# A mixer layer's TensorE stream rewritten: transposed projections, one attention slot per pair, and the softmax division on VectorE

## What is computed

```
(qa, ka, va, za, qb, ckv, iq, ik, iw, zb, qc, kc, vc, zc, ga, gb, gc) = _split_cols(h @ w_in[l])
ckv = _rmsnorm(ckv, ckv_g[l])
ya = _mixer_a(qa, ka, va, sink[l], t5_bias) * jax.nn.silu(za)
yb = _mixer_b(qb, ckv, iq, ik, iw, w_uk[l], w_uv[l], t5_bias) * jax.nn.silu(zb)
yc = _mixer_c(qc, kc, vc, c_rel_bias[l]) * jax.nn.silu(zc)
merged = (jax.nn.sigmoid(ga) * (ya @ w_pa[l]) + jax.nn.sigmoid(gb) * (yb @ w_pb[l])
          + jax.nn.sigmoid(gc) * (yc @ w_pc[l]))
x = x + merged @ w_o[l]
return _rmsnorm(x, final_g)
```

## Time and profile before

| what | value |
|---|---|
| median of 3 runs | 1018.62 us |
| lowest, highest | 1018.24, 1019.21 us |
| the profiled execution's own time | 1018.98 us |
| its span | 1017.2 us |
| mean granted TensorE clock | 0.996 of full |
| busy: TensorE, VectorE, ScalarE, GpSimd | 98%, 56%, 46%, 10% |
| moved by DMA | 187.01 MB, mean 184 GB/s |

### The profile page before, as it was taken

The page is one execution under the profiler, slowest core; times in us unless marked ns, Lnnn a source line. Parts: engine busy times, 40 slices in busy tenths (PEclk is TensorE's granted clock), DMA queues, the critical chain, the costliest instruction groups (busy, mean ns, idle before and its releaser), DMA issues.

```text
span 1017.2 us, 14153 instructions
## 1 busy us (share of the span) xinstructions
PE 1001.8 (98%) x4835; PEld 827.3 (81%) x4835; DVE 573.2 (56%) x954; ACT 469.8 (46%) x757; POOL 101.3 (10%) x125
## 2 busy tenths in 40 slices
PE   8999999999999999999999999999999999999995
PEld 6887888888888888888888888888888888888884
DVE  6656555555655555655645557566456545545652
ACT  6554444444444445543544455445434434444441
POOL 1000211111110300221211002211000000000000
PEclk9999999999999999999999999999999999999998
DMA  9765555555555555555556555555455865555452
GB/s 307 243 207 172 172 180 187 169 173 160 164 175 175 176 166 176 188 174 175 161 184 182 166 176 187 169 174 164 156 195 166 316 220 188 189 181 186 166 197 92
DMA packets 106218, 187.01 MB, mean 184 GB/s; under 512 B 12752, under 2 KB 24096, under 8 KB 105536
## 3 DMA queue, kind: packets, MB, share of 16 engines
q1 hardware_dynamic: 105792, 186.21, 57.0%
q0 software_dynamic: 240, 0.24, 0.1%
q10 hardware_dynamic: 144, 0.01, 0.0%
HBM read 184.26 MB, written 2.17 MB: 183 GB/s over the span
## 4 chain that ended last, share of the span: by engine, by line
PE 97%; DMA 1%; DVE 0%; SPq 0%; issue 0%; ACT 0%; POOLq 0%; DVEq 0%; POOL 0%
PE bank L1010 29%; PE bank L1012 29%; PE bank L1011 28%; PE bank L984 4%; PE bank L1033 2%; PE bank L1147 1%; PE bank L1049 1%; PE bank L1050 1%; PE bank L1048 1%; DMA raw<-in_w_in_dram 1%; PE bank L1122 0%; SPq L329 0%; PE bank L1086 0%; PE bank L1085 0%; PE bank L1084 0%; DVE act L975 0%
## 5 line engine op out<-in xcount | busy, mean ns | idle before, releaser
L703 DVE TENSOR_TENSOR w_lo<-raw,w_hi 128x1024 fp32r<-128x1024 f32 (+1 forms) x324 | 400.8, 1252 | 279.9 <-ACT w_hi L502 278.5
L1010 PE MATMUL bank<-w_hi,h_hi 128*128 128x512 f32 x1088 | 436.0, 401 | 2.5 <-DVE w_lo L703 2.5
L502 ACT ACTIVATE w_hi<-raw 128x1024 fp32r<-128x1024 f32 (+1 forms) x324 | 336.0, 1050 | 209.2 <-PE bank L1012 190.6
L1012 PE MATMUL bank<-w_hi,h_lo 128*128 128x512 f32 x1088 | 425.0, 391 | 0.0
L1011 PE MATMUL bank<-w_lo,h_hi 128*128 128x512 f32 x1088 | 423.7, 389 | 0.0
L1010 PEld LDWEIGHTS bank<-w_hi,h_hi 128*128 128x128 f32 x1088 | 204.4, 188 | 44.6 <-issue 3.1
L1012 PEld LDWEIGHTS bank<-w_hi,h_lo 128*128 128x128 f32 x1088 | 204.2, 188 | 44.1
L1011 PEld LDWEIGHTS bank<-w_lo,h_hi 128*128 128x128 f32 x1088 | 204.7, 188 | 39.6
L438 POOL TENSOR_TENSOR biasmask<-bias,masks 128x512 f32<-128x512 f32 (+1 forms) x48 | 65.2, 1378 | 245.3 <-DMA bias<-bias_table 241.0
L1010 PE MATMUL bank<-w_hi,y_hi 128*128 128x512 f32 x192 | 76.4, 398 | 0.0
L1012 PE MATMUL bank<-w_hi,y_lo 128*128 128x512 f32 x192 | 75.0, 390 | 0.0
(11 more groups left out here) (152 smaller groups left out, 578.8 us busy)
## 6 DMA issues: line engine op xcount, KB each, us to landing
raw<-in_w_in_dram SPq DMA_DIRECT2D x232, 512.0 KB, 4.3
raw<-in_w_o_dram SPq DMA_DIRECT2D x32, 512.0 KB, 4.2
raw<-in_w_pa_dram SPq DMA_DIRECT2D x16, 512.0 KB, 3.6
raw<-in_w_pb_dram SPq DMA_DIRECT2D x16, 512.0 KB, 3.6
raw<-in_w_pc_dram SPq DMA_DIRECT2D x16, 512.0 KB, 4.5
bias<-bias_table SPq DMA_DIRECT2D x24, 256.0 KB, 4.9
raw<-in_w_in_dram SPq DMA_DIRECT2D x16, 256.0 KB, 5.9
act<-in_x_t_dram SPq DMA_DIRECT2D x8, 256.0 KB, 6.4
```

The source lines that it names most:

```text
L502: nc.scalar.activation(w_hi[:, s, 0:n], raw[:, s, 0:n], ACT.Copy).then_inc(hi_ready, 1)
L703: nc.vector.tensor_tensor(w_lo[:, s, 0:n], raw[:, s, 0:n], w_hi[:, s, 0:n].bitcast(F32), ALU.subtract).then_inc(lo_ready, 1)
L1010: mm(acc, xh, wh[:, e, :], start=first, stop=False)
L1012: ins = mm(acc, xl, wh[:, e, :], start=False, stop=last)
```

## The change

All loops are unrolled, and pieces come in a new order, packed on the host into one array `w_s` (4 KB contiguous per partition and piece); biases with branch A's and C's masks are laid out on the host too, one load of 393 KB per pair.

- `CHUNKS`: q, z, k of branch C and the indexer's q are computed transposed (`cols_step`): weights stationary, 128 columns, and 256 columns of h moving; a piece is 4 k-tiles by 256 output columns (2 by 512 for iq), 24 products. The expansion of the latent (uk, uv) becomes streamed pieces. There are 330 pieces: g 96, q 48, z 48, P 48, o 32, k 16, v 16, kvc 8, iq 8, ik 4, uk 4, uv 2; those of uk have 12 products of 256.
- `slots`: TensorE attends once per pair, in slot i after a given piece: P times V of pair i-1, scores of pair i+1, transposes of pair i. P times V has v (64 columns) stationary and 128 columns of P's transpose moving, so y comes out transposed, one head on each half of the partitions. Slots stand 6 to 16 pieces apart.
- VectorE divides the probabilities by their sum before they are transposed (4 `tensor_scalar` per pair), and multiplies P times V by the SiLU path when it leaves PSUM.
- The first two chunks use x scaled by the gain alone; for the rest x is multiplied by the norm's factor on GpSimd (`x_scaled`), where also the sums of squares are added and the power of a 128 by 256 row tile is taken, and split again on ScalarE and VectorE.
- The first piece is loaded and split in halves; x's first part comes by ScalarE's queue; the warm-up is 13 products of 512.

The diff, cut to its core:

```diff
-BR = 10
-KINDS = ["q", "q", "i"] + ["q"] * 10 + ["z", "z", "g", "P", "g", "P", "g", "P", "g", "P"] * 3 + ["o"] * 4
-PIECES = [8, 8, 4] + [8] * 10 + [8, 8, 8, 4, 8, 4, 8, 4, 8, 4] * 3 + [8] * 4
+CHUNKS = ([("kvc", 0, 0), ("iq", 0, 0), ("ik", 0, 0)] + quarters("q", 0) + quarters("z", 0)
+          + [k for u in range(4) for k in (("q", 1, u), ("uk", 0, u))]
+          + [("q", 2, 0), ("uv", 0, 0), ("q", 2, 1), ("uv", 0, 1), ("q", 2, 2), ("q", 2, 3)]
+          + quarters("k", 0) + [("v", 0, 0), ("v", 0, 1)] + quarters("z", 1)
+          + branch(0) + quarters("z", 2) + branch(1) + branch(2) + quarters("o", 0))
+KINDS = [k for k, _, _ in CHUNKS]
+PIECES = [{"uk": 1, "uv": 1, "kvc": 8, "iq": 8, "v": 8, "g": 8, "o": 8}.get(k, 4) for k in KINDS]
...
+def slots():
+    yield -1, FIRST[AT["z", 0, 3]]
+    for i, key in enumerate((("q", 1, 0), ("q", 1, 2), ("q", 2, 0), ("q", 2, 2), ("k", 0, 0), ("k", 0, 2),
+                             ("v", 0, 0), ("v", 0, 1))):
+        yield i, FIRST[AT[key]] + 2
+    for b in range(2):
+        yield 8 * b + 8, FIRST[AT["z", b + 1, 0]] + 2
+        for k in range(7):
+            yield 8 * b + 9 + k, FIRST[AT["g", b, 0]] + 2 + 6 * k
+    yield 24, FIRST[AT["g", 2, 0]] + 1
...
+            def parts(g, n):
+                return [w[:, g % RING, 0:width(g)].rearrange("p (k n) -> p k n", n=n) for w in (w_hi, w_lo)]
+            def cols_step(g, c, e, kt, n_kt, hi_t, lo_t):
+                n_blk = 4 if KINDS[c] == "iq" else 2
+                wh, wl = parts(g, n_blk * P)
+                for n in range(n_blk):
+                    cols = slice(n * P, (n + 1) * P)
+                    acc = bank[2 * (c % 2) + n][:, 0:SEQ]
+                    mm(acc, wh[:, e, cols], hi_t[:, kt, :], start=kt == 0, stop=False)
+                    mm(acc, wh[:, e, cols], lo_t[:, kt, :], start=False, stop=False)
+                    ins = mm(acc, wl[:, e, cols], hi_t[:, kt, :], start=False, stop=kt == n_kt - 1)
+                return ins
...
+            def product(c, j, hi_t, lo_t):
+                g = FIRST[c] + j
+                kind = KINDS[c]
+                step, n_kt = (cols_step, 4) if kind in "qkz" else (cols_step if kind in ("iq", "uk") else rows_step, 2)
+                pe.wait_ge(lo_ready, g + 1)
+                for e in range(n_kt):
+                    ins = step(g, c, e, n_kt * j + e, n_kt * PIECES[c], hi_t, lo_t)
                 ins.then_inc(used, 1)
...
-            def attend(k, br, m):
-                a = pair(br, m)
...
+            def attend(i):
+                p = i - 1
+                if p >= 0:
+                    pe.wait_ge(pT0_copied, p + 1)
...
+                    for blk, t, kt, first, last in ((0, 1, 0, True, False), (1, 1, 1, False, True),
+                                                    (2, 0, 0, True, True)):
+                        for h in range(2):
+                            ins = mm(bank[4 + t][HD * h:HD * (h + 1), SROW:CH], v_cols(p, kt, h),
+                                     probsT[:, h, blk * P:(blk + 1) * P], start=first, stop=last)
+                    ins.then_inc(pv_ready, 1)
+                p = i + 1
+                if p < NPAIR:
...
+                    wait(pe, biased, 4 * p)
                     for t in (1, 0):
                         for h in range(2):
                             r = slice(HD * h, HD * (h + 1))
                             cols = t_of(t)
+                            ins = mm(bank[4 + h][:, cols], qT[p // 8][r, p % 8, t * P:(t + 1) * P],
+                                     k_rows(p)[r, 0:cols.stop - cols.start], start=True, stop=True)
                     ins.then_inc(scored, 1)
+                if 0 <= i < NPAIR:
+                    pe.wait_ge(norm_ready, 4 * i + 4)
+                    wait(pe, pT0_copied, i)
+                    wait(pe, pT1_copied, i)
...
-            for _ in range(WARM_COLD):
+            zero = h_hi[:, 0:2, :].rearrange("p k t -> p (k t)")
+            for _ in range(WARM_COLD + 4):
                 mm(bank[3][:, :], zero[:, 0:P], zero, start=True, stop=True)
+            pe.wait_ge(lo_half, 1)
+            pe.wait_ge(uT_lo, 1)
+            rows_step(0, 0, 0, 0, KT, u_hi, u_lo)
+            pe.wait_ge(lo_ready, 1)
+            pe.wait_ge(uT_lo, 2)
+            rows_step(0, 0, 1, 1, KT, u_hi, u_lo).then_inc(used, 1)
...
+                        if j == 3:
+                            pe.wait_ge(sq_sum, 5)
+                            pe.wait_ge(zeroed, 1)
+                            for t in range(NT):
+                                mm(bank[6][:, 2 * t:2 * t + 2], squares[:, t * P:(t + 1) * P], ones[:, 0:2],
+                                   start=True, stop=True)
+                            mm(bank[7][:, 0:SEQ], ones[:, :], squares[:, 0:SEQ], start=True, stop=True
+                               ).then_inc(ssq_row, 1)
...
+            pool.wait_ge(row_mean, 1)
+            nc.gpsimd.tensor_tensor(rstd_row[:, :], mean_row[:, :], neg_half[:, :], ALU.pow).then_inc(row_rstd, 1)
+            pool.wait_ge(row_mean, 2)
+            nc.gpsimd.tensor_tensor(rstd[:, 0, :], mean_sq[:, 0, :], neg_half[:, 0:NT], ALU.pow
+                                    ).then_inc(rstd_ready, 1)
+            pool.wait_ge(row_rstd, 1)
+            pool.wait_ge(uT_lo, KT)
+            for k in range(4):
+                xs = x_cols(4 * k, 4).rearrange("p (k s) -> p k s", k=4)
+                nc.gpsimd.tensor_tensor(xs, xs, rstd_row[:, :].unsqueeze(1).to_broadcast([P, 4, SEQ]), ALU.mult
+                                        ).then_inc(x_scaled, 1)
...
+                if g - 4 in SLOT_AT:
+                    p = SLOT_AT[g - 4] + 1
+                    if p < NPAIR:
+                        ve.wait_ge(exp_ready, 5 * p + 5)
+                        nc.vector.tensor_tensor(denom[:, :, :], expsum[:, :, :], sink_exp[:, :, :], ALU.add
+                                                ).then_inc(denom_ready, 1)
+                        ve.wait_ge(denom_ready, p + 1)
+                        nc.vector.reciprocal(r_denom[:, :, :], denom[:, :, :]).then_inc(rdenom_ready, 1)
+                        ve.wait_ge(rdenom_ready, p + 1)
+                        for h in range(2):
+                            for t in (1, 0):
+                                s = scores[:, h, t_of(t)]
+                                nc.vector.tensor_scalar(s, s, r_denom[:, h, t:t + 1], None, ALU.mult
+                                                        ).then_inc(norm_ready, 1)
...
+                    if i >= 1:
+                        p = i - 1
+                        ve.wait_ge(pv_ready, p + 1)
+                        wait(ve, scored, min(i + 2, NPAIR))
+                        for t in range(NT):
+                            cols = slice(P * t, P * (t + 1))
+                            nc.vector.scalar_tensor_tensor(
+                                qT[p // 8][:, p % 8, cols], bank[4 + t][:, SROW:CH], 0.25,
+                                silu[:, p % 8, cols], ALU.mult, ALU.mult).then_inc(y_ready, 1)
...
+            def load(g):
+                s, n = g % RING, width(g)
+                wait(sp, lo_ready, g - RING + 1)
+                sp.dma_start(raw[:, s, 0:n], w_s[g, :, 0:n]).then_inc(raw_in[s], 16)
+            def load_bias(p):
+                wait(sp, biased, 4 * (p - 1))
+                sp.dma_start(bias_t[:, p % 2, :, :], bias[p].rearrange("p (h n) -> p h n", h=2)
+                             ).then_inc(bias_in[p % 2], 16)
...
+            sp.dma_start(raw[:, 0, 0:CH], w_s[0, :, 0:CH]).then_inc(raw_half, 16)
+            sp.dma_start(raw[:, 0, CH:2 * CH], w_s[0, :, CH:2 * CH]).then_inc(raw_in[0], 16)
+            for j in range(1, 8):
+                sp.dma_start(x_cols(2 * j, 2), x_t[:, 16 + 2 * SEQ * j:16 + 2 * SEQ * (j + 1)]).then_inc(xT_in[j], 16)
+                load(j)
```

More of the change, by code:

```diff
@@ L92, in bucket, with hybrid_trunk @@
     return 24 + log_bucket(rel - 1, 8, 4, 64) if rel > 0 else log_bucket(-rel, 24, 12, 128)
[L95 to L109, removed]
+def hybrid_trunk(nc, x, x_t, w_s, bias, ckv_g, sink, final_g, out):
     x_v = x[0].rearrange("(t p) n -> p t n", p=P)
     out_v = out[0].rearrange("(t p) n -> p t n", p=P)
-    ZCOL = [COL["za"], COL["zb"], COL["zc"]]
-    GCOL = [COL["ga"], COL["gb"], COL["gc"]]
     with ExitStack() as ctx:
@@ L178, in hybrid_trunk @@
[L178 to L187, removed]
@@ L321, in _ @@
         def _(sp):
-            def load(g, src, width=CH, part=0):
-                s = g.base % RING
-                if part == 0:
-                    wait(sp, lo_ready, g.of(lambda n: n - RING + 1))
-                kts, w = src.shape[1], src.shape[2]
-                slot = raw[:, s, 0:kts * width].rearrange("p (k n) -> p k n", k=kts)
-                sp.dma_start(slot[:, :, part:part + w], src).then_inc(raw_in[s], 16)
-            def load_chunk(g, view, col, n):
-                for j in range(n):
-                    load(g + j, view[:, 2 * j:2 * j + 2, ds(col, CH)])
@@ L757, in hT_group @@
```

(20 more changed lines are left out.)

1409 lines of the change are left out of this document (625 added, 784 removed).

## The result

| | before | after |
|---|---|---|
| median (lowest to highest), us | 1018.59 (1018.24 to 1019.21), 4 runs | 1042.04 (1041.2 to 1042.89), 4 runs |
| profiled span, us | 1017.2 | 1041.1 |
| forecast, us | | 999.8 (984 to 1022) |
| TensorE busy | 98% | 95% |
| chain that ended last on TensorE | 97% | 90% |

The ratio after to before is 1.023, interval 1.0212 to 1.0247. The forecast missed the range and the sign.

What follows compares the result with a forecast made beforehand. TensorE's own instruction stream was taken to bound the kernel. Changes to it of -18.4 us, start -3.2 and stalls +2.8 gave -18.8; 1018.98 - 18.8 - 0.36 = 999.8 us, range 984 to 1022.

Steps and rivals of the forecast that it cites:

- (1), (2): Transposed projections on TensorE, 256-column products at 0.117 us: +8.7 us; k,v expansion moved into streamed pieces: net -4.5 us.
- products of 512 columns: TensorE's uninterrupted wide products, priced at 0.228 us each throughout, rounded up for the few behind each interruption.
- (5), (6): P times V with v stationary, 1.05 us for 1.33 per pair: -6.7 us; one interruption per pair: nothing further gained.
- first product: TensorE's start: first product at 7.0 us instead of 9.00, -2.0 us, and a later hole gone, -1.2 us.
- division: VectorE's multiplies moved before the transposes, under 1.4 us per pair; with slack of 5.7 us, cost nothing.
- stalls of TensorE: Waits on x's new normalization before q: 2.2 us, plus 0.6 for VectorE's split of h; +2.8 us.
- What is moved, and its cover: Step on x's new normalization chain through VectorE, GpSimd and ScalarE before q, part hidden behind iq and ik: +2.8 us.
- T: Time of GpSimd's 128x256 power: taken as 4 us, free up to 1.8, each further microsecond a stall.
- rival B: GpSimd's power makes the kernel slower once T reaches 22.8 us; 1063 us at T = 67; chance 0.11.
- warm-up bound: Four warm-up products, 128x128 weights with 256 columns: three steps of 0.114 us, the low end for narrow products.
- Rival C: TensorE's weight load not hidden behind 256 columns: 0.15 us each, 1097 us; decides from 0.1234; chance 0.04.
- rival D: No change, 1018 us: the division makes each of 23 slots wait 0.8 us; chance 0.04.

Runs made afterwards that it cites:

- e5_nodiv: e2_diag without VectorE's four multiplies of a pair by the inverse sum (a 128x1 memset stands in): 1002.06 us, ratio 0.9836.
- e3_powidle: Kernel before plus three GpSimd powers of 128x16, 128x64 and 128x128 that nobody waits for: 1018.62 us against 1019.18, ratio 0.9992.
- e1_mult: Changed kernel with GpSimd's 128x256 power replaced by a multiply, so the norm factors are wrong: 1002.37 us, ratio 0.9832.
- e2_diag: Changed kernel without the wide power: GpSimd's 128x2 power spread by VectorE's diagonal, a TensorE product with ones and ScalarE's copy; 1002.48 us, ratio 0.983.
- e7_dveadds: e2_diag with the five additions of squares moved from GpSimd to VectorE, between iq's first pieces: 998.9 us, ratio 0.9805.
- e4_micro: Kernel before with six warm-up groups of 24 products on zeros, various widths: 0.1196 us each at 256 columns with weights 128 wide.
- e8_dvescale: e7_dveadds with the multiply of x by its norm factors also moved from GpSimd to VectorE: 998.2 us, ratio 0.9799.
- e6_pvserial: e2_diag with P times V of a pair done head by head instead of alternating heads: 1008.98 us, ratio 0.9908.

## Why the prediction was wrong, by its own steps

| term | forecast, us | measured, us | off by |
|---|---|---|---|
| (1), (2) products of 256 columns | 0.117 each | 0.120 each | +9.7 |
| products of 512 columns | 0.228 | 0.227 | -2.4 |
| (5), (6) one slot: P times V, scores, six transposes | 2.75 | 2.47 | -6.4 |
| first product | 7.0 | 7.05 | 0 |
| division | 0 | 0 (e5_nodiv) | 0 |
| stalls of TensorE, with the clock after them | 2.8 | 44.5 | +41.7 |
| sum | 999.8 | 1042.0 | +42.6 of 42.2 |

**The step that failed** is in "What is moved, and its cover": "I take T = 4, near the row of its size, since one that it resembles in width is a better guide than an extrapolation by 128". T was 42.3. The mechanism, its place and the point from which it decides (T = 22.8) stand there as rival B. B's own sum with the measured T is 42.3 - 1.8 + 0.6 = 41.1 of stall against 21.6 of gain, 1038. It was the price that I got wrong, and with it B's chance of 0.11. The two rows said so, had I weighed them otherwise. In the earlier trace rows a plain operation on 2 elements takes 0.19 and a power on 2 elements 0.71 on the same engine. They differ in the operation and in the instruction's form (one tensor input against two); e3_powidle has a multiplication of two tensors of 128x2, 0.19 us as well, so the 0.52 belongs to the power. The 1.31 us of a plain operation on 256 elements says what a plain operation adds with width, and nothing of the power. No row held a power of any other width, so the range of T was 1.3 to 67 with something like an even chance on either side of 22.8, and the range of the time should have reached to 1063. I had both ends of T written down, and ended the range at a T near 24. e1_mult shows that with T at a plain operation's price the time is 1002.4.

**The cover.** I let q be the first to be late, with ik's 5.6 us of products in between. Late first was ik, because the splits of its weights stand on both engines behind the wait for the little power, and that one stood behind the wide one. I had costed the little power's 0.7 us and not what waits for it. Here it moved nothing much: ik's products then ran from 94.89, beside the multiplication of x, which q waited for anyway.

**What wasn't in the sum at all**: the additions of the squares on GpSimd (20.55 to 32.05). I costed the squares on TensorE and passed over them. They made the wait of 2.4 us in after, and in e2_diag one of 2.7 and a clock of 0.83 over the next 10; moving them gave some 3 us back (e7_dveadds). Of the 44.5 in the table 37.2 is the big hole, 2.6 this one, and the rest is the clock after both, a wait of 0.7 before q and one of 0.35 at 10 us.

**Narrow products.** The chain (after) in a stretch of 160 with one row of scores among them:

```profile
179.86 0.12 PE bank L927
...
193.41 0.85 PE bank L979 x8
194.27 0.32 PE bank L926
...
200.09 0.12 PE bank L928
```

20.23 us less 0.85 and the 0.20 behind it are 19.18, 0.1199 each; with those behind interruptions, 0.1203 over all 2928. It was the upper end that I gave (0.120). I had taken ik's price for weights 72 wide to hold for 128. e4_micro has 0.1167 for 72 and 0.1196 for 128. My warm-up bound (three steps of 0.114 from a row of four) was too short a row for the third decimal: 24 of the same take 0.1196 each. The Trainium skill, "TensorE: Matmul & The Clock Gate", section LDWEIGHTS, gives a load as its columns over 1.2, an estimate of 107 ns for 128. The 0.111 at 192 columns is near it. The 0.1196 at 256 is above both that and the stream's half of 0.2275, so load and stream don't seem to lie fully beside each other; why isn't shown. Rival C decided from 0.1234 and so didn't happen.

**Right.** P times V: 0.81 against my 0.85 and 0.20 behind. The 0.20 came once, not twice, since transposes follow the scores in a slot, and they take 0.81 where 0.65 was. The first product: 7.05 against 7.0. The division (rival D): I had its end 10.7 us after the slot and a slack of 5.7; it was 12.0 and 6.0. Put the measured stalls aside and the rest of the sum is off by 0.9 us; with them small, the kernel lands 2.6 us above 999.8 (e1_mult, e2_diag).

## What to carry to other kernels

Price an operation by its own kind before its width: where the only row of that kind is at another size, keep both readings, fixed and per element, and let the chance of each follow from the rows of that kind alone. When work goes to an engine with slack, ask what stands behind it on that engine, and who waits for that: here two engines waited for 0.7 us of work that stood behind 42.3. And GpSimd's slack isn't free to fill: its additions stretch VectorE's operations at that moment, while the same work on VectorE cost nothing that shows.

## What the runs showed of the hardware

- GpSimd's power in f32 on 128 partitions: 0.70, 3.69, 10.6, 21.2 and 42.3 us for 2, 16, 64, 128 and 256 columns (after, e3_powidle). Its multiplication takes 0.19 for 2 (e3_powidle) and 1.72 for 256 (e1_mult).
- VectorE's operations with two inputs in SBUF wait for GpSimd's additions (5.03 us for 0.89 of work, after) and multiplications (two splits of 128x288 from 92.09 on took 5.21 us in after; in e8_dvescale, where GpSimd doesn't multiply, one takes 0.46), and not for its power (e3_powidle). So did one with a single input: the negation of 128x48 took 1.19 us beside the multiplications (after) and 0.18 in e8_dvescale. Four with one input from PSUM did not: 1.41 us from 97.22 on in after, still beside them, and 1.42 in e8_dvescale.
- Weights 128 wide: 0.1196 us a product at 256 columns, and 0.111 at 192 with no other compute engine at work (e4_micro).
- Passes of 128 columns with weights 64 wide: 0.0675 us alternating between the halves of the output partitions, 0.089 one half after the other (e2_diag, e6_pvserial).
- After TensorE's waits of 2.4 and 37 us the granted clock fell to its lower level, 1.2 GHz: products of 512 columns took 0.43 us in place of 0.23 from 30.86 to 33.42, and those of 256 took 0.21 in place of 0.12 from 94.89 to 99.19. After the first wait six products ran at the full clock before it fell. A wait doesn't always bring it: in e1_mult TensorE waited 2.5 us at the same place, and the clock stayed at 1.00.
